# An encoder step on one core: where two attention programs load first, and the block order of the third

## The reference, cut to what matters

```python
s = jnp.einsum('bqhgd,bkhd->bhgqk', qg, k).astype(F32) * (d ** -0.5)
s = s.reshape(b, hq, tq, -1) + bias
s = jnp.where(mask, s, NEG_INF)
p = jax.nn.softmax(s, axis=-1)
o = jnp.einsum('bhgqk,bkhd->bqhgd', p, v)
```

## Time and profile before

| | us |
|---|---|
| median of 3 runs (lowest, highest) | 4377.17 (4371.15, 4381.04) |
| profiled execution, its own time | 4374.29 |
| its span, first to last instruction | 4372.5 |
| PE busy in the span | 3836.7 (88%) |
| mean granted TensorE clock | 0.945 |

### The profile page before, as it was taken

The page is one execution under the profiler, slowest core; times in us unless marked ns, Lnnn a source line. Parts: engine busy times, 40 slices in busy tenths (PEclk is TensorE's granted clock), DMA queues, the critical chain, the costliest instruction groups (busy, mean ns, idle before and its releaser), DMA issues. The chain is left out here.

```text
span 4372.5 us, 51419 instructions
## 1 busy us (share of the span) xinstructions
PE 3836.7 (88%) x18129; PEld 2643.7 (60%) x18129; DVE 2250.8 (51%) x4858; ACT 1593.5 (36%) x2424; POOL 682.4 (16%) x408
## 2 busy tenths in 40 slices
PE   5999999968888999996998779889877699999698
PEld 3789988966666566564874544443344455555376
DVE  7211111137776444443230199999678876666332
ACT  3100001104444334333320189995345333333333
POOL 3100000011212111111430000000032632211133
PEclk8999999989999999998999899999979799999899
DMA  5221122133334223212431211111243210100243
GB/s 184 69 73 67 63 73 81 65 84 82 92 91 99 63 60 74 64 36 91 160 126 63 63 38 57 56 58 48 80 104 94 61 39 23 25 21 3 97 154 125
DMA packets 222512, 328.51 MB, mean 75 GB/s; under 512 B 22224, under 2 KB 129032, under 8 KB 220896
## 3 DMA queue, kind: packets, MB, share of 16 engines
q1 hardware_dynamic: 173280, 236.21, 18.9%
q10 hardware_dynamic: 43776, 72.50, 4.5%
q0 software_dynamic: 5216, 16.70, 1.8%
HBM read 214.35 MB, written 110.99 MB: 74 GB/s over the span
## 5 line engine op out<-in xcount | busy, mean ns | idle before, releaser
L1017 PE MATMUL attAB_p_o<-attAB_pt,attAB_v 128*65 128x512 f32 (+3 forms) x1120 | 441.3, 492 | 3.0 <-ACT attAB_pt L1064 3.0
L1104 DVE TENSOR_REDUCE attAB_mx<-attAB_p_s 128x1 f32<-128x512 f32 (+2 forms) x360 | 210.7, 608 | 313.1 <-PE attAB_p_s L952 200.6
L497 DVE COPY ab_stage<-ab_pA 128x256 f32<-128x256 f32 (+1 forms) x108 | 56.5, 523 | 603.5 <-PE ab_pA L466 579.4
L2360 DVE TENSOR_SCALAR_CACHE_REDUCE cd_junk<-score,cd_thr 128x512 bf16<-128x512 f32 (+8 forms) x288 | 350.3, 1274 | 1.4 <-DVE cd_thr L2377 0.3
L2398 ACT ACTIVATE cd_gate<-score,cd_thr 128x384 bf16<-128x384 f32 (+2 forms) x192 | 322.3, 1679 | 23.3 <-DVE cd_thr L2377 16.1
L994 PE MATMUL attAB_p_t<-attAB_q_a,attAB_k_a 128*128 128x512 f32 (+3 forms) x560 | 314.0, 564 | 0.0
L464 PE MATMUL ab_pA<-ab_W_hi,h_hi 128*128 128x256 f32 x1088 | 309.0, 284 | 3.3 <-PE ab_pA L466 3.2
L465 PE MATMUL ab_pA<-ab_W_lo,h_hi 128*128 128x256 f32 x1088 | 307.9, 283 | 0.0
L466 PE MATMUL ab_pA<-ab_W_hi,h_lo 128*128 128x256 f32 x1088 | 307.8, 283 | 0.0
L495 ACT ACTIVATE ab_stage<-ab_pA 128x256 f32<-128x256 f32 (+1 forms) x108 | 50.1, 464 | 700.3 <-PE ab_pA L466 669.5
L1625 PE MATMUL attD_p_o<-attD_pt,attD_v 128*65 128x512 f32 x548 | 287.6, 606 | 0.0
(11 more groups left out here) (343 smaller groups left out, 8809.4 us busy)
## 6 DMA issues: line engine op xcount, KB each, us to landing
attAB_raw<-t_k SPq DMA_DIRECT2D x32, 640.0 KB, 7.3
attAB_raw<-t_q SPq DMA_DIRECT2D x32, 640.0 KB, 9.7
t_qg<-cd_stage SPq DMA_DIRECT2D x74, 256.0 KB, 2.0
ab_W_raw<-in_w_ab SPq DMA_DIRECT2D x17, 1024.0 KB, 5.8
mix_o<-t_o SPq DMA_DIRECT2D x34, 512.0 KB, 4.3
t_q<-ab_stage ACTq DMA_DIRECT2D x40, 256.0 KB, 2.0
t_k<-ab_stage ACTq DMA_DIRECT2D x40, 256.0 KB, 2.0
norm_x<-in_x ACTq DMA_DIRECT2D x17, 512.0 KB, 3.6
```

What stands on the lines that cost most here:

```text
L1017: done = nc.tensor.matmul(p_o[u % 2][0:VW, i0 * P:(i0 + n) * P], left, pt[c % NPT][:, at * P:(at + n) * P], start=(c == plan.chunks_of[u][ ...
L2360: nc.vector.tensor_scalar(junk[nth % 2][:, 0:widths[n]], sc[n][:], T[:, n:n + 1], None, ALU.is_ge, ALU.add, accum_out=cnt[s % 2][:, n:n + ...
```

## The change

In attention A and B, SP issues identity, keys, then bias; ACT issues the queries of head 0 on its own queue as its first work; PE turns the bias before it waits for the set-up; DVE sets only the first buffers at the start and does those of the second (`fix_second`) one piece a chunk in the first six chunks. In C and D, SP issues identity, keys, bias and sinks (or 16-bit identity), then masks and other keys; ACT issues the queries of the first two blocks as its first work. D takes its blocks in the order 5, 4, 6 to 16, 3, 2, 1, 0; units 0 and 1 (block 5) are the early ones, and a mask is not turned before the last chunk but one of the block two places ahead.

```diff
@@ attention_by_keys, SP
                 sp.dma_start(ident[:], d.ident).then_inc(ident_in, 16)
+                item_loads(sp, 0, 0)
                 for h in range(NH):
                     if kinds[h] == "A":
                         bias_loads(sp, h)
                     for n in range(ITEMS):
-                        item_loads(sp, h, n)
+                        if h or n == 2:
+                            item_loads(sp, h, n)
@@ PE
                 pe.wait_ge(ident_in, 16)
+                turn_bias(0)
                 pe.wait_ge(fixed, FIXED)
                 pe.wait_ge(ident_kept, 2)
-                turn_bias(0)
@@ ACT
+                item_loads(act, 0, 1)
                 for n in range(ITEMS):
                     round_item(act, 0, n)
@@ DVE
+                def fix_second(x):
+                    if x < 3:
+                        nc.vector.memset((k_b, c_b, q_b)[x][1][HD:AUX, :].bitcast(F32), 1.0).then_inc(second_fixed, 1)
+                    elif x == 3:
+                        nc.vector.memset(v[1][:, :, HD:VW], 1.0).then_inc(second_fixed, 1)
+                        nc.vector.memset(v_c[1][:, :, HD:VW], 1.0).then_inc(second_fixed, 1)
+                    else:
+                        tile = (k_b, c_b)[x - 4]
+                        dve.wait_ge(second_fixed, x - 3)
+                        nc.vector.tensor_scalar(tile[1][HD:AUX, :], tile[1][HD:AUX, :].bitcast(F32), shown[HD:AUX, 0:1], None,
+                                                ALU.mult).then_inc(second_fixed, 1)
...
-                for j in pair:
-                    nc.vector.memset(k_b[j][HD:AUX, :].bitcast(F32), 1.0).then_inc(fixed, 1)
...
+                nc.vector.memset(k_b[0][HD:AUX, :].bitcast(F32), 1.0).then_inc(fixed, 1)
...
                 for c in range(NT):
                     if c + 2 < NT and kind_of(c + 2) == "A":
                         add_bias(c + 2)
+                    if c < 6:
+                        fix_second(c)
@@ D's order, BlockPlan
-BLOCK_ORDER = list(range(NB))
+BLOCK_ORDER = [5, 4, *range(6, NB), 3, 2, 1, 0]
-        self.early = [u for u in range(len(self.units)) if due[u] <= 0]
+        self.early = [u for u in range(len(self.units)) if due[u] <= 0 or u < 2]
                 begin = max(due[u - 1], 0)
+                if p >= 2:
+                    begin = max(begin, self.chunks_of[2 * p - 3][-1] - 1)
@@ attention_by_blocks, SP
                 sp.dma_start(ident[:], d.ident).then_inc(consts, 16)
+                key_loads(sp, 0)
                 sp.dma_start(bias[:], (d.bias_c if kind == "C" else d.bias_d).rearrange("h p n -> p h n")).then_inc(consts, 16)
...
-                key_loads(sp, 0)
-                query_loads(sp, 0)
                 if kind == "D":
                     for b in range(NMASK):
                         mask_loads(sp, b)
-                query_loads(sp, 1)
                 for m in range(1, len(items)):
                     key_loads(sp, m)
@@ ACT
+                query_loads(act, 0)
+                query_loads(act, 1)
                 act.wait_ge(fixed, FIXED)
                 round_keys(0)
```

More of the change, by code:

```diff
@@ L782, in attention_by_keys @@
         bias_in = [sem(f"bias_in{k}") for k in pair]
-        ident_in = sem("ident_in")
+        ident_in, second_fixed = sem("ident_in"), sem("second_fixed")
         ITEMS = 3
-        FIXED = 2 * 5 + 2 + 2 + 4
+        FIXED = 5 + 2 + 2 + 2
+        SECOND = 5 + 2
         span = lambda h: plan.last_of_head[h] + 1 - plan.first_of_head[h]
@@ L846, in split_queries @@
             j, m = h % 2, ITEMS * h + 1
+            if h == 0:
+                dve.wait_ge(fixed, FIXED)
+            if h == 1:
+                dve.wait_ge(second_fixed, SECOND)
             dve.wait_ge(rounded, m + 1)
@@ L931, in maximum @@
                         pe.wait_ge(q_split, h + 1)
+                        if h == 1:
+                            pe.wait_ge(second_fixed, SECOND)
                         if h == HEADS:
@@ L1163, in output @@
                                             ).then_inc(o_out, 1)
-                for j in pair:
-                    nc.vector.memset(k_b[j][HD:AUX, :].bitcast(F32), 1.0).then_inc(fixed, 1)
[L1167 to L1170, removed]
+                nc.vector.memset(k_b[0][HD:AUX, :].bitcast(F32), 1.0).then_inc(fixed, 1)
+                nc.vector.memset(q_b[0][HD:AUX, :].bitcast(F32), 1.0).then_inc(fixed, 1)
                 for k in pair:
@@ L1175, in _ @@
                 dve.wait_ge(ident_in, 16)
+                nc.vector.tensor_copy(ident_r[:], ident[:]).then_inc(ident_kept, 1)
                 nc.vector.tensor_reduce(shown[HD:AUX, :], ident[HD:AUX, HD:FORGET], AX.X, ALU.max).then_inc(ident_kept, 1)
[L1177 to L1184, removed]
+                nc.vector.memset(c_b[0][HD:AUX, :].bitcast(F32), 1.0).then_inc(fixed, 1)
+                nc.vector.memset(v[0][:, :, HD:VW], 1.0).then_inc(fixed, 1)
+                nc.vector.memset(v_c[0][:, :, HD:VW], 1.0).then_inc(fixed, 1)
+                dve.wait_ge(ident_kept, 2)
+                dve.wait_ge(fixed, FIXED - 2)
+                for tile in (k_b, c_b):
+                    nc.vector.tensor_scalar(tile[0][HD:AUX, :], tile[0][HD:AUX, :].bitcast(F32), shown[HD:AUX, 0:1], None,
+                                            ALU.mult).then_inc(fixed, 1)
                 keep_bias(0)
@@ L1279, in __init__ @@
                 begin = max(due[u - 1], 0)
+                if p >= 2:
+                    begin = max(begin, self.chunks_of[2 * p - 3][-1] - 1)
                 steps = due[u] - begin
+                assert steps > 0
                 turn = [(p, k) for k in turns(p)]
```

## The result

The changed kernel takes 4391.32 us (median of 16 runs, 4382.73 to 4402.16) against 4376.97 us (16 runs, 4369.05 to 4384.51): the ratio is 1.0033, 95% interval 1.0024 to 1.0043. It is slower by about 14 us, where 14 us faster was forecast, and lies 3 us above the range's end of 4388. The profiled execution has a span of 4389.4 us, 16.9 more than before's 4372.5.

The account below looks back on a forecast made before the run. PE was taken to bound D's large blocks, while small ones paid more per chunk. Terms +1 (A, B), +9 (C), -2 and -22 (D) sum to -14: 4360 from the profiled 4374.29, forecast 4363 as median; range 4343 to 4388.

Parts of the forecast that it names:

- +9 forecast: Attention C starts 9 us later, as PE and DVE wait for the bias behind the keys; ends 0 and +11.
- the 14.5: Delay of C's and D's constants in us: keys 5.8, queries' share 1.5 and 2.3, values 4.9.
- A and B, +1 forecast: Attention A and B: PE starts 2 us earlier, second buffers' set-up charged 3, net +1 us; ends -6 and +7.
- about 5.4 of it fit into idle time, and I charge 3: A and B: of 9.4 us second-buffer set-up on DVE in the first six chunks, 5.4 hide and 3 are charged.
- My end of the range for this, +7: A and B's upper end: +7 us if none of the second buffers' set-up fits into DVE's idle time.
- D's loop, -22 forecast: D's six small blocks, 0 to 5, take 117.8 us against 139.6, so -22; ends -44 and +8.
- 45.6 + 22.3 = 67.9: D's loop: blocks 5 and 4 at 22 chunks of 2.07 us, 45.6, plus a cold start of 22.3.
- 49.9: D's loop: blocks 3 to 0, taken last, cost 49.9 us in place of 79.6.
- three signs: Signs of error: C's constants under 8 us later; D's last four blocks over 73 us; blocks 5 and 4 over 85.
- D's start, -2 forecast: D's first score 2 us earlier, as POOL prepares one early block, 11.3 us, not two; ends -10 and +5.
- the tail without a lead: Rival, chance 0.18: D's last blocks 3 to 0 lack cover and cost their old 79.6 us; sum +16, 4393.
- That transfers do not take turns: Rival, chance 0.20: SP's and ACT's queues do not alternate by packet, bias follows keys at once; sum -31, 4346.
- DVE as D's bound in any order: Rival, chance 0.22: DVE bounds D whatever the block order, the loop gains nothing; sum +8, 4385.

Follow-up runs that it names:

- e7: Kernel before plus D's new order, both load moves in C and D, and DVE splitting the first keys before waiting for the constants: 4366.76 us, 0.9976 to before.
- e6: Kernel before plus D's new order and, in C and D, keys ahead of the bias with queries still on SP's queue: 4361.26 us, 0.9969 to before.
- e5: Kernel before plus D's new order and, in C and D, first two blocks' queries on ACT's queue, bias still ahead of keys: 4360.14 us, 0.9956 to before.
- e3: Kernel before with only D's block order and its plan changed, all loads as before: 4362.98 us, 0.9964 to before.
- e12: Kernel before with D's order 4, 5, 6 to 16, 3, 2, 1, 0, POOL's preparation in two-head pieces, C's keys ahead of bias: 4362.73 us, 0.9964 to before.
- e4: Kernel before with only the loads of C and D changed, D's order and A, B as before: 4386.32 us, 1.0028 to before.
- e9: Kernel before plus D's new order, loads as before, each POOL preparing operation in four pieces of two heads: 4361.97 us, 0.9963 to before.
- e2: Kernel before with only A and B changed, but the second buffers' set-up done at the start before DVE keeps the bias: 4377.47 us, 1.0003 to before.

## Why the prediction was wrong

**C was right**, in size and mechanism: +9 forecast, +8.9 measured, by constants 14.3 us later (14.5) and queues that take turns. e7 shows the chain. The shares of keys, queries and values in the 14.5 were not tried one by one with all three in the queues; alone, the keys made it 5.1 (e6) and the queries 0.5 (e5).

**A and B, +1 forecast, +10.6 measured.** The step that failed is "about 5.4 of it fit into idle time, and I charge 3". PE busy 8.88 and DVE busy 6.43 of 10 us were read as room for DVE's pieces. But DVE's idle time there was the other half of a ping-pong: PE fills a bank, DVE reduces it, PE may go on. A piece of 1.8 or 1.9 us in DVE's queue puts the next reduction off, and PE waits 2.88 and 3.10 us; and after each of these waits it works at the lower clock, for which the sum had no term. By the shift rows the pieces, 8.1 us in all (5.5 of memsets, 2.6 of products, the last of these still to come), have cost 10.8: 6.1 of waits and 4.7 of slower work. My end of the range for this, +7, did not hold it either.

**D's loop, -22 forecast, -5.6 measured.** Two of the three terms were right: blocks 5 and 4 took 67.5 (45.6 + 22.3 = 67.9), blocks 3 to 0 took 45.7 (49.9). The third was not written as a term: that blocks 6 to 16 keep their 546.8 us. They took 567.6: block 16 15.1 us more, block 15 5.0, the rest 0.7. The rate of 2.07 us a chunk is that of chunks with their neighbours' fills, masks and preparation in them, and the last block before, at 55.7 us for 34 chunks, had none. What the small blocks seemed to overpay, 3.32 against 2.07, was in good part work for blocks behind them. The stretches above and the earlier trace rows give the account: blocks 0 to 5 became 26.4 us shorter (139.6 to 113.2), by 14.5 of PE's busy time and 11.9 of its idle time; blocks 6 to 16 became 20.8 longer, by 13.6 of busy and 7.2 of idle time. The earlier trace rows had the warning: of 139.6 us PE was busy 114.4, so a gain of 22 had to take nearly all of the 25.2 us in which it was idle. None of the three signs that the prediction names for being wrong came up (constants 14.3 us later, not under 8; blocks 5 and 4 in 67.5, not over 85; the last four in 45.7, not over 73): they watch the parts that moved, and none the blocks that were to stay as they were.

**D's start, -2 forecast, +1.7 measured**, within its ends. The constants (14.4 later, 14.5 forecast) and POOL's start (25.8 us into the stage, 25.7 forecast) came as forecast. The step that was too small is POOL's preparation of the one block, 14.0 us in place of 11.3 (its copy alone 4.86 beside DVE's key split, 2.84 in e3); and from the end of the cached keys' split to the first score it was 11.0 in place of 10. Against e3, whose order alone gives -8.5, the two moves of the loads take 10.3, of which 5.0 are POOL's later start.

**The rivals.** The total lies near that of the tail without a lead, 4393, but not by its mechanism: the four blocks took 45.7 us, and it needed 73. That transfers do not take turns is refuted (193 to 190), and with it the strict reading of the Trainium skill that the prediction puts beside that rival: C's constants come at 12.5 us in e6 and 15.2 in e12, with the queries on SP's queue, and at 21.4 in e4, with them on ACT's. DVE as D's bound in any order comes nearest for the loop, with gain 0; but e9 takes 25 us off DVE's busy time in the loop (469.1 to 443.6) and PE's 636 stay, with 4 us less between them, so mostly PE's work bounds it. The misses are 9.6 in A and B, 16.4 in D's loop and 3.7 at its start, 29.7 of the 30.9 us between the sum's -14 and the trace's +16.9.

## What to carry to other kernels

Price a reordered loop by the work of the bound engine and by its idle time, not by chunks times a rate: where work is done ahead, a rate holds neighbours' work, and the block that comes last is cheap because it has none. Idle time of an engine that alternates with the bound engine is no room for new work, and a wait there can cost more than its length, if the bound engine comes back at the lower clock; look for a gap in which nobody waits for it, such as the 8.9 us before the bias that e2 fills. Two moves of loads that are harmless alone can together put the one transfer on which the chains wait behind all the others.

## What the hardware showed unexpectedly

A DVE cast of 128 x 4 elements, 0.17 us at its shortest, lasted 4.16 us beside one POOL operation and 5.36 us beside a run of POOL's pieces of some 1.15 us each. The Trainium skill, SBUF — State Buffer, section Who interferes with whom, says that of a DVE instruction in a 2-port mode, which a cast can enter, and a POOL instruction, the one that issues first holds the shared ports for its whole instruction. e3's row agrees in that the cast ends with POOL's operation, to 0.02 us; which of the two issued first it does not show, for the cast's row begins 0.07 us before POOL's. e9's first row shows that DVE need not get its turn between POOL instructions that follow at once; in the other row the cast ended with the copy's last piece, ahead of the additions (1.13 us). When it gets its turn was not tried.

A standstill of PE of 2.88 or 3.10 us, in attention A and B of the changed kernel, was followed by work at the lower clock: the granted clock is 0.54 from 993.04 to 996.50 and 0.50 from 1000.19 to 1006.50. In e2 waits of 0.60 to 0.70 us in the same places left the clock at 1.00.
